# Inverse square roots of a hybrid encoder block: a power operation of GpSimd instead of Newton steps on VectorE

## The reference, cut to what matters

```
def rms_norm(x, g):
    xf = x.astype(jnp.float32)
    y = xf * lax.rsqrt(jnp.mean(xf * xf, axis=-1, keepdims=True) + NORM_EPS)
    return (y * g.astype(jnp.float32)).astype(x.dtype)
...
    # in rwkv7_group
    kk = kk / jnp.maximum(jnp.sqrt(jnp.sum(kk * kk, axis=-1, keepdims=True)), 1e-12)
    ...
    yn = ((y - mean) * lax.rsqrt(var + GN_EPS)).reshape(T, B, H * N)
...
    # in reference
    xn = rms_norm(h, norm1_g[i])
    ...
    h = h + cross_attn(rms_norm(h, norm2_g[i]), rms_norm(mem, mem_norm_g[i]), wq_x[i], wkv_x[i], wo_x[i])
    h = h + moe(rms_norm(h, norm3_g[i]), router_w[i], router_b[i], moe_w1[i], moe_b1[i], moe_w2[i], moe_b2[i])
return rms_norm(h, final_g)
```

## Time and profile before

| | |
|---|---|
| median of 3 runs | 1257.74 us (1257.34 to 1260.52) |
| the profiled execution, its time | 1261.86 us |
| its span, first to last instruction | 1260.1 us |
| mean granted clock of TensorE | 0.993 of full speed |
| TensorE busy | 1206.4 us, 96% |
| VectorE busy | 311.1 us, 25%, 771 instructions |
| ScalarE busy | 197.2 us, 16% |
| GpSimd busy | 14.2 us, 1%, 56 instructions |
| moved by DMA | 445.52 MB, 354 GB/s over the span |

### The profile page before, as it was taken

How to read it: one execution, slowest core, us unless ns; L and a number is a source line. 1 busy time by engine, 2 the same in 40 slices (tenths; PEclk the granted TensorE clock), 3 DMA queues, 4 the chain that set the end, 5 groups by cost and what they waited for, 6 DMA issues and landing times.

```text
span 1260.1 us, 17481 instructions
## 1 busy us (share of the span) xinstructions
PE 1206.4 (96%) x7452; PEld 578.8 (46%) x7452; DVE 311.1 (25%) x771; ACT 197.2 (16%) x371; POOL 14.2 (1%) x56
## 2 busy tenths in 40 slices
PE   7989989999999999999999999999999999999997
PEld 6778778888843333333333333332333333333333
DVE  4764155113322112112111211211111211111212
ACT  2313143012211111111111111111111111111101
POOL 4000000000000000000000000000000000000000
PEclk9999999999999999999999999999999999999999
DMA  9343203864889999999999999999999999999995
GB/s 325 119 127 109 69 8 130 348 252 191 330 314 425 429 405 432 432 432 432 431 433 432 433 432 431 431 432 432 432 431 431 433 432 432 433 433 433 425 425 209
DMA packets 29923, 445.52 MB, mean 354 GB/s; under 512 B 8433, under 2 KB 8817, under 8 KB 11441
## 3 DMA queue, kind: packets, MB, share of 16 engines
q1 hardware_dynamic: 24944, 443.74, 83.8%
q10 hardware_dynamic: 4928, 1.05, 0.4%
HBM read 443.47 MB, written 1.31 MB: 353 GB/s over the span
## 4 chain that ended last, share of the span: by engine, by line
PE 71%; DMA 25%; ACT 2%; issue 1%; DVE 1%; SPq 0%; DVEq 0%; ACTq 0%
PE ps L1503 21%; DMA ring<-in_moe_w 15%; PE ps L1543 14%; PE ps L959 10%; DMA arena<-in_moe_w 9%; PE ps L980 7%; PE ps L1447 4%; PE ps L1421 3%; PE ps L1406 2%; PE ps L1435 1%; ACT arena L907 1%; PE ps L1161 1%; PE ps L987 1%; PE ps L1440 1%; DMA ring<-in_w_in 1%
## 5 line engine op out<-in xcount | busy, mean ns | idle before, releaser
L1503 PE MATMUL ps<-ring,arena 128*64 128x512 f32 x1248 | 273.6, 593 | 13.8 <-DMA ring<-in_moe_w 13.2
L1503 PE MATMUL ps<-arena 128*64 128x512 f32 x792 | 174.0, 593 | 9.0 <-DMA arena<-in_moe_w 9.0
L1503 PEld LDWEIGHTS ps<-ring,arena 128*64 128x64 f32 x1248 | 88.9, 137 | 194.2 <-issue 173.2
L1543 PE MATMUL ps<-ring,arena 128*64 128x512 f32 x576 | 127.7, 595 | 0.0
L899 ACT ACTIVATE arena<-arena 128x512 f32<-128x512 f32 x31 | 19.5, 630 | 679.3 <-DVE arena L2103 679.3
L2103 DVE TENSOR_SCALAR arena<-ps 128x512 f32<-128x512 f32 x31 | 21.4, 692 | 397.7 <-PE ps L1503 397.7
L959 PE MATMUL ps<-arena,ring 128*128 128x256 f32 x480 | 111.4, 393 | 7.4 <-DMA ring<-in_w_in 7.4
L1503 PEld LDWEIGHTS ps<-arena 128*64 128x64 f32 x792 | 56.4, 137 | 123.9 <-issue 109.6
L959 PEld LDWEIGHTS ps<-arena,ring 128*128 128x128 f32 x480 | 93.7, 197 | 22.6 <-issue 7.6
L1543 PE MATMUL ps<-arena 128*64 128x512 f32 x408 | 90.8, 595 | 1.8 <-DMA arena<-in_moe_w 1.8
L2116 DVE COPY arena<-ps 128x512 f32<-128x512 f32 x32 | 22.1, 692 | 236.4 <-PE ps L1543 236.4
(11 more groups left out here) (308 smaller groups left out, 875.1 us busy)
## 6 DMA issues: line engine op xcount, KB each, us to landing
ring<-in_moe_w SPq DMA_DIRECT2D x51, 4096.0 KB, 35.7
arena<-in_moe_w SPq DMA_DIRECT2D x32, 4096.0 KB, 37.1
arena<-in_moe_w SPq DMA_DIRECT2D x12, 2048.0 KB, 28.0
ring<-in_moe_w SPq DMA_DIRECT2D x11, 2048.0 KB, 32.8
ring<-in_w_in SPq DMA_DIRECT2D x12, 1024.0 KB, 5.2
ring<-in_wkv_x SPq DMA_DIRECT2D x8, 1024.0 KB, 4.8
ring<-in_w_out SPq DMA_DIRECT2D x4, 1024.0 KB, 4.7
ring<-in_wq_x SPq DMA_DIRECT2D x4, 1024.0 KB, 7.1
```

Of the source, the lines that this page charges most:

```text
L1503: ins = t.matmul(ps[c * BLK:(c + 1) * BLK, 4 + b, :], xeT[:, col:col + BLK], w(k % 4)[:, f0:f0 + 512], start=False, stop=(k == KC - 1), sk ...
L1543: ins = t.matmul(ps[c * BLK:(c + 1) * BLK, 7, :], src[:, col:col + BLK], w(k // 2)[:, f0:f0 + 512], start=(k == 0), stop=(k == KC - 1), sk ...
```

## The change

At all nine places the guess and the Newton steps go. VectorE (for key too) makes the mean plus epsilon and raises the semaphore `means_ready`. GpSimd, in its queue behind the constants, waits for its nine turns in a fixed order (x, mem, key, head, group, h, tile0, tile1, out), raises the numbers to the power -0.5 in place, by one `tensor_tensor` with a column of -0.5, and raises `roots_ready`. Whoever uses the root waits for that: VectorE at x, mem, head, group, h, tile0, tile1 and out, TensorE at key, ScalarE at out. Two instructions are new in GpSimd's first part: a memset of that column, and the wait for `ksum` before `X16` is replaced by X16's place behind the key root.

```
+        ROOTS = ("x", "mem", "key", "head", "group", "h", "tile0", "tile1", "out")
+        def rooted(eng, name):
+            eng.wait_ge(sem("roots_ready"), ROOTS.index(name) + 1)
...
+            def inverse_roots(name, v):
+                rows, n = v.shape
+                pool.wait_ge(sem("means_ready"), ROOTS.index(name) + 1)
+                g.tensor_tensor(v, v, power[0:rows, :].to_broadcast([rows, n]), ALU.pow).then_inc(sem("roots_ready"), 1)
+            link(g.memset(power[:, :], -0.5))
             link(g.memset(ident[:, :], 0.0))
...
-            product(pool, "ksum")
+            inverse_roots("x", st[:, 2:4])
+            inverse_roots("mem", st[:, 0:2])
+            inverse_roots("key", krs[0:NH, :])
             link(g.memset(X16[:, :, :], 0.0))
             g.affine_select(out=X16[:, :, :], in_=X16[:, :, :], compare_op=ALU.not_equal, fill=1.0, base=0,
                             pattern=[[1, SUB], [-1, SUB]], channel_multiplier=0).then_inc(sem("X16_unit"), 1)
+            inverse_roots("head", st[:, 8:16])
+            inverse_roots("group", st[:, 16:32])
+            inverse_roots("h", st[:, 4:6])
+            for i in range(NT):
+                inverse_roots(f"tile{i}", st[:, 6 + i:7 + i])
+            inverse_roots("out", st[:, 36:38])
...
-            act.wait_ge(sem("out_rstd_ready"), 2)
+            rooted(act, "out")
...
-            pe.wait_ge(sem("knorm_ready"), 1)
+            rooted(pe, "key")
...
-            def rstd(c0, c1, width, eps):
+            def rstd(name, c0, c1, width, eps):
                 x = st[:, c0:c1]
-                link(v.tensor_scalar(x, x, 1.0 / width, eps, ALU.mult, ALU.add))
-                rsqrt(x, x, wk[:, 0:c1 - c0], wk[:, 32:32 + c1 - c0])
+                v.tensor_scalar(x, x, 1.0 / width, eps, ALU.mult, ALU.add).then_inc(sem("means_ready"), 1)
+                rooted(dve, name)
...
             dlink(v.tensor_scalar(krs[0:NH, :], o[0:NH, 0:T], 1e-24, None, ALU.max), "ksum")
-            rsqrt(krs[0:NH, :], krs[0:NH, :], kra[0:NH, :], krb[0:NH, :])
-            dve.sem_inc(sem("knorm_ready"), 1)
+            dve.sem_inc(sem("means_ready"), 1)
             shift(1)
...
             def rstd_last(i):
                 dve.wait_ge(sem("most_squares_ready"), i + 1)
-                most, x, y, s2 = (st[:, c + i:c + i + 1] for c in (40, 44, 6, 46))
-                link(v.tensor_scalar(x, most, -0.5 / D, -0.5 * EPS, ALU.mult, ALU.add))
-                link(v.scalar_tensor_tensor(out=x, in0=st[:, 42 + i:43 + i], scalar=-0.5 / D, in1=x, op0=ALU.mult, op1=ALU.add))
-                link(v.tensor_scalar(y.bitcast(I32), x.bitcast(I32), -0.5, 519526879.0, ALU.mult, ALU.add))
-                for _ in range(3):
-                    link(v.scalar_tensor_tensor(out=s2, in0=y, scalar=y, in1=x, op0=ALU.mult, op1=ALU.mult))
-                    link(v.scalar_tensor_tensor(out=y, in0=s2, scalar=1.5, in1=y, op0=ALU.add, op1=ALU.mult))
+                most, x = (st[:, c + i:c + i + 1] for c in (40, 6))
+                link(v.tensor_scalar(x, most, 1.0 / D, EPS, ALU.mult, ALU.add))
+                v.scalar_tensor_tensor(out=x, in0=st[:, 42 + i:43 + i], scalar=1.0 / D, in1=x, op0=ALU.mult, op1=ALU.add)\
+                 .then_inc(sem("means_ready"), 1)
+                rooted(dve, f"tile{i}")
...
             dve.wait_ge(sem("out_stat_ready"), 2)
-            x, r, s2 = st[:, 34:36], st[:, 36:38], st[:, 38:40]
-            link(v.tensor_scalar(x, st[:, 32:34], -0.5 / D, -0.5 * EPS, ALU.mult, ALU.add))
-            link(v.tensor_scalar(r.bitcast(I32), x.bitcast(I32), -0.5, 519526879.0, ALU.mult, ALU.add))
-            for _ in range(3):
-                link(v.tensor_tensor(s2, r, r, ALU.mult))
-                link(v.tensor_tensor(s2, s2, x, ALU.mult))
-                link(v.scalar_tensor_tensor(out=r, in0=s2, scalar=1.5, in1=r, op0=ALU.add, op1=ALU.mult))
-            dve.sem_inc(sem("out_rstd_ready"), 2)
+            v.tensor_scalar(st[:, 36:38], st[:, 32:34], 1.0 / D, EPS, ALU.mult, ALU.add).then_inc(sem("means_ready"), 1)
+            rooted(dve, "out")
```

More of the change, by code:

```diff
@@ L252, in program @@
         st = sb("st", [P, 64])
+        power = sb("power", [P, 1])
         lam = sb("lam", [P, 8])
@@ L1637, in _ @@
             two = lambda x: x.rearrange("p (a b) -> p a b", a=2)
-            def rsqrt(y, x, s1, s2):
-                link(v.tensor_scalar(s1, x, -0.5, None, ALU.mult))
-                link(v.tensor_scalar(y.bitcast(I32), x.bitcast(I32), -0.5, 1597463007.0, ALU.mult, ALU.add))
-                for _ in range(3):
-                    link(v.tensor_tensor(s2, y, y, ALU.mult))
-                    link(v.tensor_tensor(s2, s2, s1, ALU.mult))
-                    link(v.scalar_tensor_tensor(out=y, in0=s2, scalar=1.5, in1=y, op0=ALU.add, op1=ALU.mult))
-            def rstd(c0, c1, width, eps):
+            def rstd(name, c0, c1, width, eps):
                 x = st[:, c0:c1]
-                link(v.tensor_scalar(x, x, 1.0 / width, eps, ALU.mult, ALU.add))
-                rsqrt(x, x, wk[:, 0:c1 - c0], wk[:, 32:32 + c1 - c0])
+                v.tensor_scalar(x, x, 1.0 / width, eps, ALU.mult, ALU.add).then_inc(sem("means_ready"), 1)
+                rooted(dve, name)
             def spread(nm, c0, diag):
-                rstd(c0, c0 + NT, D, EPS)
+                rstd(nm, c0, c0 + NT, D, EPS)
                 for i in range(NT):
@@ L1926, in _ @@
             dve.wait_ge(sem("osq_ready"), 1)
-            rstd(8, 16, P, EPS)
+            rstd("head", 8, 16, P, EPS)
             dve.sem_inc(sem("osr_ready"), 1)
@@ L1934, in _ @@
             dve.wait_ge(sem("ysq_ready"), 1)
-            rstd(16, 32, HD, GN_EPS)
+            rstd("group", 16, 32, HD, GN_EPS)
             for i in range(NT):
@@ L1978, in _ @@
             dve.wait_ge(sem("stat_ready"), 2)
-            rstd(4, 6, D, EPS)
+            rstd("h", 4, 6, D, EPS)
             link(v.tensor_scalar(st[:, 36:38], st[:, 4:6], XSCALE, None, ALU.mult))
```

## The result

The changed kernel takes 1285.68 us (1284.33 to 1288.98, 4 runs), against 1258.05 us (1257.34 to 1260.52, 4 runs) of the kernel before: a ratio of 1.0216, with a 95% interval of 1.0198 to 1.0233, or 27.6 us slower. The profiled execution took 1284.33 us.

What follows compares the result with a forecast made beforehand. The expert-weight DMA stream, timed by TensorE's work before expert 0, was taken as the bound. Only the last root's 1.5 us gain counted, all else hidden: median 1257.74 becomes 1256.2 us, range 1254.5 to 1270.5.

Steps and rivals of the forecast that it cites:

- Rival A: Key root: its 256-column power is dear, so the kernel is slower, 1270.2 or 1266.8 us at 100 ns per column; chance 0.21.
- A's first way: Key: the root reaches TensorE after 60.1 us, from 59 ns per column; 10.6 us late at 100 ns.
- A's second way: Key: GpSimd's power holds back VectorE's operation at 53.44 us; TensorE 14 us late at 100 ns per column.
- x: First root: the power waits for GpSimd's constants until about 18.55 us; slack 2.6 us less p, costs nothing at p = 0.4.
- mem: Second root: on an idle GpSimd, diagonals end at 29.70 us, TensorE takes them at 32.58; nothing lost or won.
- head and group: Roots before group's scalings: VectorE gains 2 x 1.7 us, but TensorE waits for a bank ScalarE clears; nothing won.
- tiles: Tile 0 and tile 1 roots: 0.56 instead of 1.5 us each, nothing won; tile 1 hurts from 1.6 us on.
- out: Last root, straight on the path: 1.5 us won, between 1.7 won and 2.1 lost.
- B: All nine places: each power has a large fixed part; 1265.5 us at p = 4; chance 0.08.
- C: At x: only the first power is dear; 1257.6 us with 4 us for it, the same; chance 0.05.
- D: All nine places: VectorE's queue is the bound, 15.6 us won, 1242.1 us; chance 0.02.
- One to one: Before expert 0: a microsecond lost or won on TensorE moves the whole DMA stream and reaches the end in full.

Runs made afterwards that it cites:

- e5: The change, with the key root laid out over 128 partitions x 64 columns and spread by a GpSimd mask product: 1257.94 us, ratio to before 1.0001.
- e4: The change, with 57 unused matmuls keeping TensorE busy in front of its wait for the key root: 1281.06 us, ratio to before 1.0200.
- e10: The change, with the key root halved: 128 columns by GpSimd power, the others by Newton on VectorE: 1267.72 us, ratio to before 1.0065.
- e1: The change, but key by Newton on VectorE again, the other eight roots by power: 1257.34 us, ratio to before 0.9998.
- e3: The kernel before, with the last root (out) alone by power on GpSimd: 1256.70 us, ratio to before 1.0001.
- e9: The change, with key packed into 64 columns and the last root's two tiles taken apart: 1258.52 us, ratio to before 1.0000.

## Why the prediction was wrong

**The forecast (1256.2 us, the same) failed at one term: the price per column of the key power.** The prediction put it at 25 ns, with an upper end of 100 ns, and got 6.4 us for the power. It is 160 ns and 41.1 us. Rival A named the place and, with the late root, the mechanism. Its bound for TensorE, 59 ns per column, was sound: in the kernel after 16.1 us lie between the power's start and the point where TensorE is ready for the root (42.38 to 58.50), 63 ns per column. But A had a chance of 0.21, its range ended at 100 ns, and only about 0.1 was left beyond. Where the prediction went astray is that it bounded an operation no row showed by multiples of the cheapest GpSimd instructions, a memset and a select. The memset's 1 ns per column told nothing of the power's 160; 1 and 100 such passes looked far apart and were not far enough. With the measured price, A's first way has the power end at 45.1 + 41.1 = 86.2 us and TensorE idle for 26.1, where it idled for 25.05; less 1.5 that makes 1282.3 us, 3.4 short of the measured time.

**A's second way did not exist.** The prediction held VectorE's operation at 53.44 back until the power's end. It ran on time. With the measured price this way comes to 86.2 - 53.44 - 3.2 - 1.5 = 28.1 us and 1285.8, next to the measured 1285.68; that is luck, for the wait that it counts isn't there. The trace of before had shown only GpSimd waiting for VectorE, and that is seen again (the first 128x32 select takes 0.86 us in the kernel after and ends at 15.13, with VectorE's sum of squares at 15.07; its repetition takes 0.21); the reverse, "the other way round", was a guess. The Trainium skill, page "SBUF — State Buffer", section "SBUF: two separate sides", has the lock held for the whole of a GpSimd instruction. For the power, e5 and the kernel after contradict this, with 0.69 us each in the middle of a power, and the measurement decides.

**A term was missing: the clock.** The prediction counted idle time at its own length. By the rows of the kernel after, 4.3 us more (1.8 + 2.5) lay in the lower clock (0.50 of full speed) behind it, of which e4 takes back 2.6; and in e10 4.63 us of idling are followed by 4.0 us of it (1.8 + 2.2).

Point by point:

- *x*: GpSimd's power ran from 18.43 to 19.15 us, where 18.55 was said, and the diagonals were there in time. The slack was smaller than counted, as TensorE was ready at 20.10 instead of 21.77 in this execution; the diagonals ended at 19.66, 0.44 us before. Hidden, as predicted, but of all the hidden places the next to cost.
- *mem*, *h*: hidden, as predicted.
- *head and group*: hidden, but dearer than said: 1.65 and 2.90 us instead of p. VectorE's scalings (to 232.5) still end before TensorE's bank is clear (233.03, with the same 0.50 us of waiting for ScalarE).
- *tiles*: "nothing won" holds for the profile that was read. At full clock tile 1 wins 0.35 us (e1 against e3), since Newton was then on the path; the slack of 0.14 us should have been read together with the clock of that stretch.
- *out*: 1.25 us were won, 1.5 said. The power of two columns takes 0.70 us, not 0.4.
- *B*, *C*: no large fixed part (0.39 us), and none for the first power (0.72 us, like the later ones of its width, 0.70). Of the 6 us that the Trainium skill (page "GPSIMD Engine Reference", section "Instruction dispatch") states for the first call of a freshly loaded kernel nothing is seen here.
- *D*: VectorE's queue bounds nothing. The 20 us taken from it came back as idling, 6.09 us for instance in front of the shift behind the key sums.
- *One to one*: right. 25.6 us later at expert 0, and 905.0 us from there to the end as in the other kernels with the new end (e1 904.8, e10 905.1).
- *The sums*: VectorE's queue loses five times 2.26, 4.6, twice 1.5 and 1.97, which is 20.9 us and not 20.6, and A's second way would bind from (56.7 - 45.1) / 256 = 45 ns per column and not 46. Neither moves the forecast.

## What to carry to other kernels

Before an operation of a kind that no row shows takes the place of cheap ones, ask what one column costs and how many columns it has: here 0.39 us + 0.16 us per column, whatever the partitions, so two columns win over ten chained instructions (0.70 against 1.97 us) and 256 lose by a factor of nine (41.1 against 4.6). If it must be there, lay the data over all partitions; that alone took the power from 41.1 to 10.5 us and the kernel back to its time before. And where a price is unknown, the rows of other kinds of instruction give a lower end only: find the breakeven (here 59 ns), and give the side beyond it a chance that doesn't rest on them.

## What was not expected

- The power of GpSimd costs 0.16 us per column, over 8 partitions as over 128: at 1, 2, 8, 16, 64, 128 and 256 columns it took 0.55, 0.70, 1.65, 2.90, 10.54, 20.71 and 41.12 us.
- TensorE's granted clock fell to 0.50 behind idling of 4.63 us as well as behind 25 us, and kb0 and kb1 then took 3.77 us instead of 1.99. Where TensorE worked through the wait, they took 1.99, but a shorter stretch of low clock followed from 86 to 90 us, whose cause is open. And behind a gap of about 3 us elsewhere the clock fell in the kernel before and not in e9.
- GpSimd's power, 41 us long, did not keep VectorE from its double-rate operations, though a GpSimd select that meets VectorE's sum of squares lasts until that ends (0.86 us here and 0.93 before, instead of 0.21; in e1 it is another select, 0.98 instead of 0.19).
